# Head 0's keys and values turned in 32x32 blocks on VectorE and regrouped through DRAM, in place of 20 TensorE transposes

## What is computed

```python
xn = rms_norm(x, norm1_g)
z = xn @ w_in + b_in          # RG-LRU input | q | k | v | o | i, f gates | merge gates A, B
ha = rg_lru(causal_dwconv(u))                      # branch A
hb = mlstm(q, k, v, i, f)                          # branch B, 4 heads of 256, chunk by chunk:
#   s = (q @ k.T) * w ; num = s @ v + e_int * (q @ C) ; C = decay * C + (wk * k).T @ v
merged = sigmoid(ga) * (ha @ w_branch_a) + sigmoid(gb) * (hb @ w_branch_b)
x = x + merged @ w_out
x = x + conv_ffn(rms_norm(x))
```

## Time and profile before

| | us |
|---|---|
| median of the runs | 1067.67 |
| the profiled execution: device time | 1067.82 |
| its span in the trace | 1066.0 |
| TensorE busy in it | 1054.0 (99%) |
| VectorE / ScalarE / GpSimd busy | 620.0 / 388.5 / 371.1 |
| the stage from projection 5 of head 0 to WA7's end | 182 to 250 |

### The profile page before, as it was taken

How to read it: one execution, slowest core, us unless ns; L and a number is a source line. 1 busy time by engine, 2 the same in 40 slices (tenths; PEclk the granted TensorE clock), 3 DMA queues, 4 the chain that set the end, 5 groups by cost and what they waited for, 6 DMA issues and landing times.

```text
span 1066.0 us, 19415 instructions
## 1 busy us (share of the span) xinstructions
PE 1054.0 (99%) x7974; PEld 1029.3 (97%) x7974; DVE 620.0 (58%) x971; ACT 388.5 (36%) x562; POOL 371.1 (35%) x180
## 2 busy tenths in 40 slices
PE   7999999999999999999999999999999999999997
PEld 6999999999999999999999999999999999999997
DVE  6777457854533343442543339999940189999413
ACT  6566787313332333232422333222211122222332
POOL 4333344333222222222223344334443344334330
PEclk9999999999999999999999999999999999999999
DMA  7433322346385592863443232322323222233312
GB/s 198 164 102 92 103 75 78 85 104 163 85 231 154 129 263 62 195 197 90 149 163 88 81 99 86 93 80 80 102 71 103 62 80 80 81 93 99 98 44 89
DMA packets 215696, 119.67 MB, mean 112 GB/s; under 512 B 39195, under 2 KB 212235, under 8 KB 215358
## 3 DMA queue, kind: packets, MB, share of 16 engines
q1 hardware_dynamic: 215404, 118.42, 39.4%
q10 hardware_dynamic: 210, 0.07, 0.0%
HBM read 97.49 MB, written 18.76 MB: 109 GB/s over the span
## 4 chain that ended last, share of the span: by engine, by line
PE 98%; ACT 1%; DMA 0%; POOL 0%; DVE 0%; issue 0%; SPq 0%; DVEq 0%
PE ring L2063 48%; PE ring L2481 22%; PE bank L2481 17%; PE bank L2353 2%; PE bank L2340 1%; PE bank L2110 1%; PE bank L2321 1%; PE bank L2333 1%; PE bank L2395 1%; PE bank L2220 1%; PE bank L2383 1%; PE bank L2418 0%; DMA x_tok<-in_x_prompt 0%; POOL x_split L917 0%; ACT sq_tok L1000 0%; PE bank L2527 0%
## 5 line engine op out<-in xcount | busy, mean ns | idle before, releaser
L2063 PE MATMUL ring<-x_split,whi 128*128 128x256 f32 (+1 forms) x2016 | 359.2, 300 | 0.0
L905 POOL TENSOR_TENSOR wlo<-stage,whi 128x1024 fp32r<-128x1024 f32 x78 | 194.2, 2490 | 411.7 <-ACT whi L963 411.7
L2063 PEld LDWEIGHTS ring<-x_split,whi 128*128 128x128 f32 x2016 | 303.9, 189 | 8.1 <-issue 7.6
L2063 PE MATMUL ring<-x_split,wlo 128*128 128x256 f32 (+1 forms) x1008 | 217.4, 297 | 0.0
L2063 PEld LDWEIGHTS ring<-x_split,wlo 128*128 128x128 f32 x1008 | 169.9, 189 | 0.0
L963 ACT ACTIVATE whi<-stage 128x1024 fp32r<-128x1024 f32 x80 | 84.3, 1054 | 92.3 <-PE ring L2063 81.2
L948 POOL TENSOR_TENSOR wlo<-stage,whi 128x1024 fp32r<-128x1024 f32 x28 | 71.7, 2560 | 108.4 <-ACT whi L1316 108.4
L2481 PE MATMUL ring<-x_split,whi 128*128 128x256 f32 (+1 forms) x512 | 88.7, 295 | 0.0
L1432 DVE SCALAR_TENSOR_TENSOR conv<-up,cols,conv 128x592 f32<-128x592 f32 x88 | 75.5, 858 | 3.1
L2481 PEld LDWEIGHTS ring<-x_split,whi 128*128 128x128 f32 x512 | 77.0, 189 | 0.0
L1969 DVE TENSOR_SCALAR conv<-up,cols 128x592 f32<-128x592 f32 x44 | 74.0, 1683 | 3.1
(11 more groups left out here) (365 smaller groups left out, 2053.3 us busy)
## 6 DMA issues: line engine op xcount, KB each, us to landing
stage<-in_w_in SPq DMA_DIRECT2D x56, 512.0 KB, 4.0
stage<-in_w_up SPq DMA_DIRECT2D x44, 512.0 KB, 3.7
stage<-in_w_down SPq DMA_DIRECT2D x16, 704.0 KB, 4.5
stage<-in_w_branch_a SPq DMA_DIRECT2D x8, 512.0 KB, 3.7
c_sample<-in_state_mlstm_C SPq DMA_DIRECT2D x16, 256.0 KB, 6.2
out_s_mlstm_C<-c_sample SPq DMA_DIRECT2D x16, 256.0 KB, 2.4
stage<-in_w_branch_b SPq DMA_DIRECT2D x8, 512.0 KB, 3.9
stage<-in_w_out SPq DMA_DIRECT2D x8, 512.0 KB, 3.8
```

The costliest lines, as they stand in the source:

```text
L905: pool.tensor_tensor(spaced(wlo[:, slot]), packed(stage[:, slot, 0:n]), spaced(whi[:, slot]).bitcast(F32), ALU.subtract).then_inc(w_lo, 1)
L2063: last = pe.matmul(of(z, t0 or -2, t1), w[:, kk * WS:kk * WS + P], x_, start=kk == 0 and m == 0, stop=kk == kn - 1 and m == 2)
```

## The change

Head 0 now takes the way of the other heads. TensorE's 20 transposes and ScalarE's four evictions go. Their turns become four VectorE instructions in the stage of WA0 to WA2, through `first_tmp`, which is `gq` and `wt[0]` (named w_t): arrays not yet in use there. Because `gates_rows` writes `gq`, it now waits for the value stores to land. SP gets sixteen stores and two loads among its loads 28 to 31. Head 0's waits for `kt[0]` and `vt[0]` become waits for those loads (`moved`), and the counts of `k_stored`, `v_stored` and `kv_turned` shift by one head.

```diff
@@ -417,6 +413,7 @@
         wt = [sb("w_t0", [P, TW], r + 1024), wt1]
         gq = sb("gate_rows", [P, TW], r + 1024 + 4 * TW)
         turn_tmp = [gq[:, :], flat(hb[:, 4:6])[:, 0:TW]]
+        first_tmp = [gq[:, :], wt[0][:, :]]
         r += 1024 + 8 * TW
         nst = sb("n_state", [P, NS, 8], r)
         misc = sb("misc", [P, 256], r + 288)
...
@@ -558,7 +551,7 @@
 
         def moved(h):
 
-            return 16 * ((h + 1) // 2)
+            return 16 * (h // 2 + 1)
 
         block = ctx.enter_context(nc.Block())
...
@@ -671,13 +664,34 @@
                     if LRU_SWAP[p] == g:
                         swap_halves(p)
 
+            def store_blocks(j, rows_, stored, turned_, blocks=turn_tmp):
+
+                sp.wait_ge(kv_turned, turned_ + j + 1)
+                for a_ in range(4):
+                    d0 = P * j + 32 * a_
+                    sp.dma_start(rows_.rearrange("(m t) d -> t m d", t=32)[:, :, d0:d0 + 32],
+                                 blocks[j][32 * a_:32 * a_ + 32, :].rearrange("p (m t) -> p m t", t=32)
+                                 ).then_inc(stored, 16)
+
+            def load_tokens(h, dst, rows_, stored, arrived):
+
+                sp.wait_ge(stored, 16 * 8 * (h + 1))
+                sp.dma_start(dst, rows_.rearrange("(c p) d -> p c d", p=P)).then_inc(arrived, 16)
+
+            for j in range(2):
+                store_blocks(j, kdram, k_stored, 0, first_tmp)
             sp.wait_ge(lc_ready, 1)
             sp.dma_start(o["p_lru_conv"][0, 0], conv_out[0:3, :]).then_inc(lru_out, 16)
             sp.dma_start(o["s_lru_conv"][0].rearrange("b j c -> (b j) c"), conv_out[3:27, :]).then_inc(lru_out, 16)
             sp.dma_start(o["p_lru_h"].rearrange("l b (f c) -> (l b f) c", c=P), h_out[0:8, :]).then_inc(lru_out, 16)
             sp.dma_start(o["s_lru_h"].rearrange("l b (f c) -> (l b f) c", c=P), h_out[8:72, :]).then_inc(lru_out, 16)
-            for g in range(28, 31):
-                main_load(g)
+            main_load(28)
+            load_tokens(0, kt[0][:, :, :], kdram, k_stored, kt_in[0])
+            for j in range(2):
+                store_blocks(j, vdram, v_stored, 2, first_tmp)
+            main_load(29)
+            load_tokens(0, vt[0][:, :, 0:DH], vdram, v_stored, vt_in[0])
+            main_load(30)
 
             def head_load(n):
...
@@ -744,40 +758,24 @@
                     sp.wait_ge(w_lo, B_WB + j - 1)
                     load(B_WB + j, (B_WB + j) % 2, wb, slice(P * j, P * j + P))
 
-            def store_blocks(j, rows_, stored, turned_):
-
-                sp.wait_ge(kv_turned, turned_ + j + 1)
-                for a_ in range(4):
-                    d0 = P * j + 32 * a_
-                    sp.dma_start(rows_.rearrange("(m t) d -> t m d", t=32)[:, :, d0:d0 + 32],
-                                 turn_tmp[j][32 * a_:32 * a_ + 32, :].rearrange("p (m t) -> p m t", t=32)
-                                 ).then_inc(stored, 16)
-
-            def load_tokens(h, dst, rows_, stored, arrived):
-
-                sp.wait_ge(stored, 16 * 8 * h)
-                sp.dma_start(dst, rows_.rearrange("(c p) d -> p c d", p=P)).then_inc(arrived, 16)
-
             for h in range(HEADS):
                 for n in range(2 if h else 3, 8):
                     if h + 1 == HEADS and n in (5, 6):
                         c_load(h, n - 1)
                     head_load(8 * (h + 1) + n)
                     if n == 6 and h + 1 < HEADS:
-                        if h:
-                            sp.wait_ge(kt_in[h % 2], moved(h))
+                        sp.wait_ge(kt_in[h % 2], moved(h))
                         for j in range(2):
-                            store_blocks(j, kdram, k_stored, 4 * h)
+                            store_blocks(j, kdram, k_stored, 4 * (h + 1))
 
                 c_load(h, 6)
                 c_load(h, 7)
                 next_load(h, 0)
                 if h + 1 < HEADS:
                     load_tokens(h + 1, kt[(h + 1) % 2][:, :, :], kdram, k_stored, kt_in[(h + 1) % 2])
-                    if h:
-                        sp.wait_ge(vt_in[h % 2], moved(h))
+                    sp.wait_ge(vt_in[h % 2], moved(h))
                     for j in range(2):
-                        store_blocks(j, vdram, v_stored, 4 * h + 2)
+                        store_blocks(j, vdram, v_stored, 4 * (h + 1) + 2)
                 sp.wait_ge(z_evicted, NZ * h + TT)
                 sp.dma_start(o["p_mlstm_C"][0, 0, h].rearrange("(i p) v -> p i v", p=P), cp[h % 2][:, :, 0:DH]
                              ).then_inc(cp_out, 16)
...
@@ -1235,10 +1218,6 @@
                     evict(t, merged[:, f, M0:], of(wide[t % 2], M0), ACT.Sigmoid, bias=cols[:, C_BGA + f:C_BGA + f + 1])
                 elif g < 24:
                     project(g - 16)
-                    if g == 21:
-                        k_tokens(0)
-                    elif g == 22:
-                        v_tokens(0)
                 elif g == 24:
 
                     act.wait_ge(lc_done, 1)
...
@@ -1705,10 +1684,18 @@
                 elif g == 23:
                     gates_log()
             evict_wa(0)
+            dve.wait_ge(tile_evicted, TILES["proj", 0, 3] + 1)
+            dve.wait_ge(lru_ps, 8)
+            for j in range(2):
+                dve.transpose(first_tmp[j], k[0][:, j, :]).then_inc(kv_turned, 1)
             gates_max()
             evict_wa(1)
+            dve.wait_ge(k_stored, 16 * 8)
+            for j in range(2):
+                dve.transpose(first_tmp[j], vf[:, j, :]).then_inc(kv_turned, 1)
             gates_sum()
             evict_wa(2)
+            dve.wait_ge(v_stored, 16 * 8)
             gates_rows()
             evict_wa(3)
             gates_inter()
...
@@ -1746,9 +1733,9 @@
 
                 dve.wait_ge(tile_evicted, TILES["proj", h, n] + 1)
                 if n == 3:
-                    dve.wait_ge(k_stored, 16 * 8 * h)
-                elif h > 1:
-                    dve.wait_ge(v_stored, 16 * 8 * (h - 1))
+                    dve.wait_ge(k_stored, 16 * 8 * (h + 1))
+                else:
+                    dve.wait_ge(v_stored, 16 * 8 * h)
                 for j in range(2):
                     dve.transpose(turn_tmp[j], src[:, j, :]).then_inc(kv_turned, 1)
...
@@ -1818,9 +1805,7 @@
                         dve.wait_ge(y_done, n + 1)
                         cpy(nt[:, c, :], Y(n)).then_inc(y_evicted, 1)
 
-                    if c == 0 and h == 0:
-                        dve.wait_ge(tile_evicted, TILES["ltok", 0] + 1)
-                    elif c == 0:
+                    if c == 0:
                         dve.wait_ge(kt_in[s], moved(h))
                     if c < 4:
                         keys(c, w[:, P - 1:P])
...
                 if 16 + n in LRU_TURN:
                     lru_gates(LRU_TURN.index(16 + n))
                 fill(0, n)
-                if n == 5:
-                    k_tokens(0)
-                elif n == 6:
-                    v_tokens(0)
-                    last_tokens(0)
             for f in range(8):
                 t = T_WA + f
                 gemm(B_WA + f, t, (B_WA + f) % 2, t % 2, KT, hh, hl, None if f else lambda kk: pe.wait_ge(lru_lo_, kk + 1))
                 if f == 0:
 
-                    pe.wait_ge(tile_evicted, TILES["ltok", 0] + 1)
+                    pe.wait_ge(lru_sig, 8)
                     for m in range(8):
                         pe.transpose(bank2(0)[0:27, P * m:P * m + P], ulast[:, m, :], ident[:, :])
                     pe.transpose(bank2(1)[0:72, 0:P], stage[:, 0, D + 224:D + 224 + 72], ident[:, :]).then_inc(lc_done, 1)
...
@@ -2326,7 +2281,7 @@
 
                     n, kap = TT * h + c, NZ * h + c
                     pe.wait_ge(p_done, n + 1)
-                    if h and c == 0:
+                    if c == 0:
                         pe.wait_ge(vt_in[s], moved(h))
                     if n >= 2:
                         pe.wait_ge(y_evicted, n - 1)
...
@@ -2362,8 +2317,7 @@
                         return
 
                     w = wt[s][:, P * c:TW]
-                    if h:
-                        pe.wait_ge(kt_in[s], moved(h))
+                    pe.wait_ge(kt_in[s], moved(h))
                     for ii in range(2):
                         pe.matmul(NU(n)[:, 16 * ii:16 * ii + 16], kt[s][:, c, P * ii:P * ii + P], w[:, LS - 1:P:LS],
                                          start=False, stop=True, skip_group_check=True)
```

More of the change, by code:

```diff
@@ L108 @@
     names = [("proj", h_ + 1, n_) for n_ in range(8)]
-    if h_ < 0:
-        names[7:7] = [("ltok", 0)]
-        names[6:6] = [("ktok", 0)]
     for name_ in names:
@@ L485, in halves @@
             return (m0, HALF), (HALF, T)
-        def turned(name):
-            return bank2(1 if name == "ltok" else 0)
         def ffn_out(n):
@@ L699, in c_load @@
                 if h + 1 < HEADS and idx >= 6:
-                    sp.wait_ge(kv_turned, 4 * (h + 1))
+                    sp.wait_ge(kv_turned, 4 * (h + 2))
```

(30 more changed lines are left out.)

## The result

The changed kernel takes **1070.8 us** (median of 12 runs, 1069.5 to 1072.4) against 1068.1 for the kernel before: ratio 1.0025, 95% interval 1.0018 to 1.0033. It is 2.7 us slower. I had forecast 1067.5 with a range up to 1070.1. The profiled execution took 1072.29 us, 1070.5 of it span.

What follows compares the result with a forecast made beforehand. TensorE was taken to bound the kernel: 2.18 us saved, 2.2 us of stall before WA7, about -0.3 net with half the chain's possible earlier start, so 1067.5 us against the profiled 1067.82; range 1065.4 to 1070.1.

Steps and rivals of the forecast that it cites:

- Bound and gain: TensorE's program in branch A: it bounds the kernel, and removing its 20 transposes takes 2.18 us off the path.
- I leave it at 203.87: Start of VectorE's eviction of WA0: unmoved at 203.87, with up to 1 us from moving low parts left in the range.
- block: VectorE and GpSimd's shared port pair: one low part of a weight stretches one VectorE piece by about 2.1 us.
- Step 2: Eight key stores on SP: 5.2 to 6.4 us, `k_stored` between 212.8 and 214.0, taken as 213.4.
- full-gain rival: Stores faster than any rows shown, idle queue before the first key store, no stall: 1065.6 us; chance 0.22.
- Step 4: Eight value stores on SP: 7.0 us, low bound 5.2, nearest row 7.7; `v_stored` at 223.4, bounds 221.5 and 224.1.
- Step 3: Load 28 on SP: issued at 213.0, 3.7 us to landing, ready at 220.2 before WA3's end at 221.6.
- Step 5: Weights for WA5 and WA6: load 29 ready at 228.5 against 228.1, load 30 at 234.8 against 234.6.
- Step 6: VectorE's gate rows: 7.1 us from 223.4, one low part falling on them, `gates_ready` at 230.5.
- Stall = `gates_ready` minus 228.3: TensorE's wait before WA7 for weight 31: `gates_ready` at 230.5 gives 2.2 us, containing load 29's 0.4 and load 30's 0.2.
- slower, by the store train: Keys and values cross DRAM in 128-byte runs amid weight loads, SP issuing nothing behind them: 1070.6 us; chance 0.13.
- two forms: Ways to `gates_ready` at 232.6: `v_stored` at 225.5 with one low part on the gate work, or 223.4 with two.

Runs made afterwards that it cites:

- repeat: The changed kernel, unaltered, run and profiled once more beside the variants: 1070.76 us, ratio 1.0026 to the kernel before; profiled execution 1069.87.
- turns early: Against the change: key turns moved ahead of VectorE's log of the gates, value turns right behind the eviction of WA0; 1066.92 us, ratio 0.9989 to the kernel before.
- the freed gate rows: Against the change: first turned block in a piece of hb, so gates_rows doesn't wait for the value stores; 1069.13 us, ratio 1.0011 to the kernel before.
- load 31 first: Against the change: load 31 issued before SP waits for gates_ready; 1069.33 us, ratio 1.0011 to the kernel before.
- both together: Against the change: loads 28, 29 and 31 all moved ahead and gates_rows freed of the value stores; 1066.82 us, ratio 0.9987 to the kernel before.

## Why the prediction was wrong

The steps beside the two profiles of the change. From each profile's times its late start is taken off (1.5 and 0.3 us, by the row of VectorE at 189.84 before):

| | forecast | first profile | repeat |
|---|---|---|---|
| eviction of WA0 starts | 203.9 | 205.9 | 205.9 |
| first key store | 205.5 | 207.4 | 207.4 |
| `k_stored` | 213.4 | 213.4 | 213.4 |
| load 28 issued | 213.0 | 213.5 | 213.5 |
| first value store | 214.3 | 214.8 | 214.8 |
| `v_stored` | 223.4 | 225.7 | 224.8 |
| `gates_ready` | 230.5 | 232.7 | 232.0 |

- **Bound and gain: right.** TensorE's 2.18 us are a microsecond each of the kernel; alone they give 2.4 between the medians and 2.2 at WA7's eviction in the profiles (250.37 to 248.54, with a start 0.3 later).
- **"VectorE has no idle time before its eviction of WA0, so ... I leave it at 203.87", with up to 1 us earlier in the range: this step failed first, and with the wrong sign.** The eviction is 2.0 us later, by one more block of 2.1 us. I had seen that the low parts move, and had priced the move only as a gain. No rival had a chain that starts late.
- **Step 2 (keys): too slow by 1.9 us.** Eight stores were issued in 4.3 us, where I took 5.8 of bounds 5.2 and 6.4; from the first store to `k_stored` it is 6.0 us and not 7.9. The rows that I had used had a load ahead; here the queue is idle, as the full-gain rival said. This error and the late start cancel, so that `k_stored` comes at the 213.4 of the forecast: luck, not a step that was right.
- **Step 4 (values 7.0, bounds 5.2 and 7.7): this is what the sum missed.** The stores took 8.0 and 9.0 us, beyond the upper bound. I had the row with the right neighbours (7.7 us) and took less than it; what the loads ahead of the stores cost stands in the series above. With 0.5 us before the first value store, where SP issues load 28 and the token load, `v_stored` is 1.4 and 2.3 us late, and `gates_ready` follows it.
- **Step 3 (load 28, "costs nothing, with 1.4 us to spare"): wrong, and a second loss of its own.** The landing took 5.8 and 6.7 us and not 3.7, with the value stores close behind it. TensorE waits for it before WA4, 1.2 and 2.1 us in the two profiles. In the change itself this lies inside the stall that `gates_ready` sets, but it is why freeing the gate rows alone still leaves 1069.1, 1.6 above the forecast.
- **Step 5 (loads 29, 30):** 29 late by 1.2 in the repeat, as a consequence of step 4. Load 30 never set a wait in the change.
- **Step 6 (gate rows 7.1 us, one block): right.** 7.0 us (227.21 to 234.19), with one block, the copy of 2.14 us at L1636. One block for one low part priced it well.
- **"Stall = `gates_ready` minus 228.3": right in form.** From `gates_ready` to weight 31 it is 13.8 us in the first profile and 13.4 in the repeat, instead of 13.2. With these the stall comes to 232.7 - 228.3 + 0.6 = 5.0 us and to 3.9 us. The waits and the slow clock were 5.0; in the repeat WA7's eviction is 4.0 us later than with the transposes alone removed (252.50 and 248.54).
- **Not in the sum at all: the clock.** After the 2.10 us wait it cost 1.8 us in one of two profiled executions. As WA7 waits for `gates_ready` anyway, it is taken out of the later waits.

Some of the prediction's own sums are off, none by enough to change its verdict. Half of 1 us is 0.5, where 0.3 is taken off. The bounds of `v_stored` leave those of step 2 out: with them they are 221.0 and 224.7, still short of what came. The full-gain rival's terms add up to `gates_ready` at 227.4, not 227.8, and without the block the sum would be 2.1 us less, not 1.9.

The rival that came is "slower, by the store train", at its 1070.6. Of its two forms the first is what the profiles show: `v_stored` near 225.5 with one block in the gate rows. The 1070.6 belongs to its second form, with two blocks, which didn't come. I gave it 0.13, for I took a price for the value stores below that of the nearest row, and did not look for a late start.

Settled by runs: the gain by itself; that the whole chain earlier brings back 3.9 of the 5.1 us (turns early); loads 28 and 29 and the gate rows as two independent supplies (the freed gate rows, load 31 first, and both together). The block moved ahead of the eviction is read in three profiles and in the run with the transposes put back. What it alone is worth of the loss was not tried apart, since the low parts can't be moved without moving TensorE; that run moves the chain 2 us and TensorE 2.2 us at once.

## What to carry to other kernels

Taking work off the bounding engine moves everything that keys on it, and so where it collides with third engines; price that move as a loss too, by looking for the instruction that the moved block will hit. A transfer's landing time holds for the neighbours it had in that row: with stores issued close behind it, it was 1.5 to 1.8 times as long. Two errors that cancel at one point of a chain hide each other there, so compare every point and not the last. And when a saving is given back as waits, look for the start of the chain first: moving the turns, the first of them by 7.5 us, gained 3.9 us with no load moved, and reordering three loads gained 3.6.

## What the runs showed of the hardware, not expected

- Adding 2.2 us of work to TensorE made the kernel 2.6 us faster (1070.76 to 1068.15).
- A wait of 2.10 us was followed by a granted clock of 0.73 over the next 6.4 us (0.50, that is 1.2 GHz, for 2.8 us of them). After waits of 0.4 to 1.6 us in this stage, in the other profiles, it stayed at 1.00.
- Eight stores in runs of 128 bytes take SP 4.3 us to issue with nothing ahead of them and 8.0 to 9.0 us right behind a weight load and a token load.
- With such stores close behind it a 512 KB weight load took 5.5 to 6.7 us to land, whether a token load stood between or not; with two token loads right behind it and no store it took 4.2. The median before was 3.7.
